# Attention values with the probabilities stationary, the row of maxima by DMA, the attention output token-major

## The reference

```python
s = jnp.einsum('bqkgd,bskd->bkgqs', qblk, k).astype(F32) * scale      # layer 0
p = jax.nn.softmax(s, axis=-1)                                       # layer 1: concatenated with the sink logit
o = jnp.einsum('bkgqs,bskd->bqkgd', p.astype(v.dtype), v)
y_a = o_a.reshape(B, T, A_W) * jax.nn.silu(a_g)
out = jnp.concatenate([y_a, y_b], axis=-1) @ w_out
```

## Time and profile before

| | |
|---|---|
| median of 3 runs | 2318.3 us |
| the profiled execution | 2322.14 us |
| its span, first to last instruction | 2320.3 us |
| mean granted TensorE clock | 0.926 |
| PE / PEld / DVE / ACT / POOL busy | 86 / 57 / 41 / 34 / 7 % |
| attention of layer 0, first scores to the gate's first load | 200.3 to 466 us |
| attention of layer 1, the same | 1192.6 to 1365.9 us |

### The profile page before, as it was taken

How to read it: one execution, slowest core, us unless ns; L and a number is a source line. 1 busy time by engine, 2 the same in 40 slices (tenths; PEclk the granted TensorE clock), 3 DMA queues, 4 the chain that set the end, 5 groups by cost and what they waited for, 6 DMA issues and landing times.

```text
span 2320.3 us, 30145 instructions
## 1 busy us (share of the span) xinstructions
PE 1995.8 (86%) x12212; PEld 1317.6 (57%) x12212; DVE 944.7 (41%) x1899; ACT 784.4 (34%) x1663; POOL 162.1 (7%) x235
## 2 busy tenths in 40 slices
PE   2988999997999988888979998968858868868998
PEld 1654555543555544765657754457457467467476
DVE  1665444212223465234634311562462461552442
ACT  2452444411222224214435531323423423423431
POOL 0000000000000000000000000014014023023000
PEclk8997999998999999998979999969979979979999
DMA  7110000031000242531010021100100100101222
GB/s 284 37 62 14 0 1 1 1 112 55 0 1 1 75 162 83 182 111 66 8 66 1 1 93 60 49 2 9 45 2 17 46 2 18 45 2 49 83 95 100
DMA packets 61292, 118.38 MB, mean 51 GB/s; under 512 B 5048, under 2 KB 27724, under 8 KB 61025
## 3 DMA queue, kind: packets, MB, share of 16 engines
q1 hardware_dynamic: 40033, 57.53, 7.4%
q0 software_dynamic: 8640, 33.75, 4.1%
q10 hardware_dynamic: 12480, 25.17, 3.0%
HBM read 96.47 MB, written 19.96 MB: 50 GB/s over the span
## 4 chain that ended last, share of the span: by engine, by line
PE 75%; DVE 10%; ACT 5%; DMA 3%; POOL 3%; DVEq 2%; issue 1%; ACTq 1%; SPq 0%; PEldq 0%; PEld 0%; POOLq 0%
PE ps L1757 8%; PE ps L535 8%; PE ps L833 8%; PE ps L1001 5%; PE ps L944 5%; PE ps L1328 3%; PE ps L1168 3%; PE ps L1353 3%; PE ps L1169 3%; PE ps L1170 3%; PE ps L788 2%; PE ps L1945 2%; PE ps L815 2%; PE ps L814 2%; PE ps L802 2%; DVE work L2045 2%
## 5 line engine op out<-in xcount | busy, mean ns | idle before, releaser
L833 PE MATMUL ps<-work 128*128 128x512 f32 (+3 forms) x512 | 232.5, 537 | 0.0
L857 DVE TENSOR_REDUCE work<-ps 128x1 f32<-128x512 f32 (+2 forms) x272 | 145.4, 561 | 201.5 <-PE ps L788 200.8
L907 ACT ACTIVATE work<-ps 128x512 f32<-128x512 f32 (+3 forms) x256 | 132.1, 517 | 195.7 <-PE ps L815 141.9
L1757 PE MATMUL ps<-hT,wring 128*128 128x512 f32 (+1 forms) x576 | 191.0, 494 | 8.0 <-SPq L2110 5.6
L535 PE MATMUL ps<-wring,hT 128*128 128x512 f32 (+2 forms) x576 | 193.0, 493 | 0.0
L814 PE MATMUL ps<-qA,kA 128*128 128x512 f32 (+3 forms) x256 | 172.3, 673 | 2.2 <-ACT work L898 1.8
L1757 PEld LDWEIGHTS ps<-hT,wring 128*128 128x128 f32 x576 | 96.2, 193 | 104.3 <-issue 100.2
L535 PEld LDWEIGHTS ps<-wring,hT 128*128 128x128 f32 x576 | 109.1, 192 | 78.5 <-issue 70.3
L1001 PE MATMUL ps<-wring,hT 128*128 128x512 f32 x288 | 127.5, 605 | 5.3 <-SPq L1547 3.4
L944 PE MATMUL ps<-hT,wring 128*128 128x512 f32 (+1 forms) x384 | 126.9, 492 | 4.0 <-DVEq L184 4.0
L788 PE MATMUL ps<-kA,qA 128*128 128x128 f32 (+3 forms) x336 | 101.6, 353 | 27.1 <-DVE work L857 14.8
(11 more groups left out here) (291 smaller groups left out, 3497.1 us busy)
## 6 DMA issues: line engine op xcount, KB each, us to landing
work<-in_w_mod ACTq DMA_DIRECT2D x10, 2048.0 KB, 13.4
work<-in_x_sample SPq DMA_DIRECT2D x16, 512.0 KB, 7.7
wring<-in_w_in_even POOLq DMA_DIRECT2D x4, 2048.0 KB, 8.9
out_y_sample<-work SPq DMA_DIRECT2D x16, 512.0 KB, 3.0
work<-out_y_sample SPq DMA_DIRECT2D x16, 512.0 KB, 4.8
wring<-in_w_in_odd POOLq DMA_DIRECT2D x3, 2048.0 KB, 8.8
wring<-in_w_in_odd POOLq DMA_DIRECT2D x12, 512.0 KB, 6.5
yA_gated<-work SPq DMA_DIRECT2D x8, 576.0 KB, 3.3
```

Source lines behind the costliest of these rows:

```text
L833: pe.matmul(ps[:, 5 + c_, (qa - q0) * P:(qb - q0) * P], vaug[:, h // 4, kt, :], pT[i % 3][:, 0:(qb - qa) * P], start=(first and l == 0), s ...
L857: v.tensor_reduce(dst, src, AX.X, ALU.max).then_inc(sm("mx_used"), 1)
L907: act.activation(pT[i % 3][:, 0:n], ps[:, ST_BANKS[i % len(ST_BANKS)], 0:n], ACT.Exp, scale=0.125).then_inc(sm("p_done"), 1)
L1757: mm = pe.matmul(ps[:, PROJ_BANK[n], 0:m], w[:, k, b * P:(b + 1) * P], hT[:, k, o:o + m], start=(k == 0), stop=(k == KD - 1))
```

## The change

The groups of query tiles become 3, 3 and 3. In "values" the operands change places: each 128 by 128 block of probabilities is stationary and the 64 values with one column of ones move, so that a product of n query tiles becomes n matmuls of 65 columns, and the output is token-major with the sum in column 64. DVE takes the reciprocal and multiplies; ACT's Ln and Exp go. In layer 1 the sink's exponential is computed by ACT from `a_nm` (128 by 9) and added by DVE, and the matmul L831 goes. The nine matmuls of "row" become one transpose of `a_nm`, one copy by ACT to `a_nmT` (9 partitions by 128), and a DMA on SP's queue that writes the nine rows one behind the other into row 64 of `qB`. The row step stands later in a head's list. `yA`, its gate (9 token tiles, 512 columns of weights moving), its DRAM copy and f_ya are token-major; fin transposes 8 blocks of 128 instead of 4 for each tile and has two pairs of banks for the result instead of three.

```diff
-        CHUNKS = [(0, 4), (4, 8), (8, 9)]
+        CHUNKS = [(0, 3), (3, 6), (6, 9)]
...
-            spread = per - (4, 6)[l]
+            spread = per - (6, 7)[l]
             for m in range(MU[l]):
                 yield "max", 0, m
-            for r in range(3):
+            for r in range(1 + l):
                 yield "row", 0, r
...
-                        elif spread < p <= spread + 3:
+                        elif spread < p <= spread + 1 + l:
                             yield "row", h + 1, p - spread - 1
...
+        def att_sp(sp, l):
+            base = l * len(PRODUCTS[0])
+            for h in range(8):
+                sp.wait_ge(sm("row_out"), 8 * l + h + 1)
+                if h >= 2:
+
+                    sp.wait_ge(sm("s_ps"), base + last_product(l, h - 2) + 1)
+                sp.dma_start(qB[h % 2][HD:HD + 1, :].bitcast(F32), a_nmT[h % 2][0:NT, :].bitcast(F32)).then_inc(sm("rows_in"), 16)
...
-                    pe.wait_ge(sm("nm_done"), 8 * l + h + 1)
-                    if r == 2:
-                        pe.wait_ge(sm("row_out"), 3 * (8 * l + h) + 1)
-                    for t in range(*ROW_TILES[r]):
-                        mm = pe.matmul(ps[HD:HD + 1, (MU[l] + r) % 2, (t - ROW_TILES[r][0]) * P:(t - ROW_TILES[r][0] + 1) * P],
-                                       a_nm[h % 2][:, t:t + 1], ident, start=True, stop=True)
-                    mm.then_inc(sm("row_ps"), 1)
+                    if r == 0:
+                        pe.wait_ge(sm("nm_done"), 8 * l + h + 1)
+                        pe.transpose(ps[0:NT, ROW_BANK, 0:P], a_nm[h % 2].bitcast(F32), ident).then_inc(sm("row_ps"), 1)
...
                     if first and c_ == 0:
-                        pe.wait_ge(sm("row_out"), 3 * (8 * l + h) + 3)
+                        pe.wait_ge(sm("rows_in"), 16 * (8 * l + h + 1))
...
                     pe.wait_ge(sm("p_done"), base + i + 1)
-                    if first and l == 1:
-
-                        pe.matmul(ps[:, 5 + c_, 0:(q1 - q0) * P], sumrow[ES, :], qB_plain[h % 2][ES, q0 * P:q1 * P],
-                                  start=True, stop=False, skip_group_check=True)
-                    pe.matmul(ps[:, 5 + c_, (qa - q0) * P:(qb - q0) * P], vaug[:, h // 4, kt, :],
-                              pT[i % 3][:, 0:(qb - qa) * P], start=(first and l == 0), stop=last,
-                              skip_group_check=True).then_inc(sm("pv_ps"), 1)
+                    for j in range(qa, qb):
+                        mm = pe.matmul(out_tile(c_, j - q0), pT[i % 3][:, (j - qa) * P:(j - qa + 1) * P], vaug[:, h // 4, kt, 0:OW],
+                                       start=(first and j == qa), stop=last, skip_group_check=True)
+                    mm.then_inc(sm("pv_ps"), 1)
...
-                    v.wait_ge(sm("ri_done"), 3 * (8 * l + h) + c_ + 1)
-                    v.tensor_tensor(yA[HD * (h % 2):HD * (h % 2) + HD, h // 2, q0 * P:q1 * P], ps[0:HD, 5 + c_, 0:(q1 - q0) * P],
-                                    a_ri[(3 * h + c_) % 2][0:HD, 0:(q1 - q0) * P], ALU.mult).then_inc(sm("y_done"), 1)
+                    nt = q1 - q0
+                    rc = a_rc[c_][:, 0:nt]
+                    v.wait_ge(sm("pv_ps"), base + last_product(l, h, c_) + 1)
+                    o = ps[:, 5 + c_, 0:nt * OW].rearrange("p (j n) -> p j n", n=OW)
+                    den = o[:, :, HD]
+                    if l == 1:
+
+                        v.wait_ge(sm("es_done"), h + 1)
+                        v.tensor_tensor(rc, den, a_es[h % 2][:, q0:q1], ALU.add)
+                        v.drain()
+                        den = rc
+                    v.reciprocal(rc, den)
+                    v.drain()
+                    v.tensor_tensor(yA[:, q0:q1, HD * h:HD * h + HD], o[:, :, 0:HD], rc.unsqueeze(2).to_broadcast([P, nt, HD]),
+                                    ALU.mult).then_inc(sm("y_done"), 1)
...
-                for k in range(KD):
-                    mm = pe.matmul(ps[:, n % 2, 0:m], w[:, k, b * P:(b + 1) * P], hT[:, k, o:o + m], start=(k == 0), stop=(k == KD - 1))
+                for k in range(KD):
+                    mm = pe.matmul(ps[:, t % 2, :], hT[:, k, t * P:(t + 1) * P], w[:, k, :], start=(k == 0), stop=(k == KD - 1))
...
-            sp.dma_start(f_yT[t % NF][:, 0:QW].rearrange("p (b n) -> p b n", b=4),
-                         yA_dram[:, :, t * P:(t + 1) * P].rearrange("b p n -> p b n")).then_inc(d, 16)
+            sp.dma_start(f_ya[t % NF], yA_dram[t * P:(t + 1) * P, :]).then_inc(d, 16)
...
-                for k in range(4):
-                    mm = pe.transpose(ps[:, t % 2, k * P:(k + 1) * P], f_y[t % NF][:, k * P:(k + 1) * P], ident)
+                for b, rows in enumerate((f_ya, f_y)):
+                    for k in range(4):
+                        mm = pe.transpose(ps[:, 2 * (t % 2) + b, k * P:(k + 1) * P], rows[t % NF][:, k * P:(k + 1) * P], ident)
...
-                    act.activation(f_yh[t % 2][:, 0:QW], f_yT[t % NF], ACT.Copy)
-                    act.wait_ge(sm("yT_ps"), NT * l + t + 1)
-                    act.activation(f_yh[t % 2][:, QW:D], ps[:, t % 2, :], ACT.Copy).then_inc(sm("yT_high"), 1)
+                    act.wait_ge(sm("yT_ps"), NT * l + t + 1)
+                    act.activation(f_yh[t % 2].rearrange("p (a n) -> p a n", a=2), ps[:, 2 * (t % 2):2 * (t % 2) + 2, :], ACT.Copy).then_inc(sm("yT_high"), 1)
```

More of the change, by code:

```diff
@@ L450, in backbone @@
         vaug = qr.take(2 * 10 * P).rearrange("p (g t n) -> p g t n", g=2, n=P)
-        yA = qr.take(4 * T).rearrange("p (b t) -> p b t", b=4)
+        yA = qr.take(NT * QW).rearrange("p (t n) -> p t n", n=QW)
         at_qkv = qr.at
@@ L472, in backbone @@
         qB = [take_rounded(ar2, f"qB{i}", T) for i in range(2)]
-        qB_plain = [Region(qB_at + i * T).take(T) for i in range(2)]
-        ES = slice(96, 97)
-        pT = [ar2.take(512) for _ in range(3)]
+        pT = [ar2.take(3 * P) for _ in range(3)]
         a_part = ar2.take(3 * NS)
         a_mx = ar2.take(NT)
-        a_nm = [ar2.take(NT) for _ in range(2)]
-        a_ri = [ar2.take(512) for _ in range(2)]
+        a_nm = [take_rounded(ar2, f"a_nm{i}", 16)[:, 0:NT] for i in range(2)]
+        a_nmT = [take_rounded(ar2, f"a_nmT{i}", P) for i in range(2)]
+        a_es = [ar2.take(NT) for _ in range(2)]
+        a_rc = [ar2.take(4) for _ in range(3)]
         ident_r = take_rounded(ar2, "ident_r", P)
         window_r = take_rounded(ar2, "window_r", 3 * P)
-        k_out = ar2.take(P)
-        assert ar2.at - P >= qr.at
-        sumrow = ar2.take(P)
+        ar2.at = max(ar2.at, qr.at + P)
+        k_out = work[:, ar2.at - P:ar2.at]
         def heads(ap, g=2):
@@ L708, in products @@
                 for c_, (qa, qb) in enumerate(CHUNKS):
[L709 to L712, removed]
-                    else:
-                        of = [(CTX, qa, qb)] + [(k, max(k - 1, qa), min(k + 2, qb)) for k in range(max(qa - 1, 0), min(qb + 1, NS))]
+                    qs = min(qb, NS)
+                    if l == 0:
+                        of = [(k, qa, qs) for k in range(NS + 1)]
+                    else:
+                        of = [(CTX, qa, qs)] + [(k, max(k - 1, qa), min(k + 2, qs)) for k in range(max(qa - 1, 0), min(qs + 1, NS))]
+                    if qb > NS:
+                        of.append((PROMPT_KEYS, NS, NT))
                     out += [(h, k, a, b, c_, i == 0, i == len(of) - 1) for i, (k, a, b) in enumerate(of)]
@@ L764, in masked, with out_tile @@
             return l == 1 and kt not in (CTX, PROMPT_KEYS)
-        ROW_TILES = [(0, 4), (4, 8), (8, 9)]
+        ROW_BANK = 1
+        assert all(m % 2 == 1 for m in MU)
+        OW = HD + 1
+        def out_tile(c_, j):
+            return ps[:, 5 + c_, j * OW:(j + 1) * OW]
+        def att_sp(sp, l):
[5 more added lines that the diff above has]
+                sp.dma_start(qB[h % 2][HD:HD + 1, :].bitcast(F32), a_nmT[h % 2][0:NT, :].bitcast(F32)).then_inc(sm("rows_in"), 16)
         def att_pe(pe, l):
@@ L886, in att_act @@
                     if r == 0:
-                        if h >= 2:
[L889 to L899, removed]
+                        act.wait_ge(sm("row_ps"), 8 * l + h + 1)
+                        if 8 * l + h >= 2:
+                            act.wait_ge(sm("rows_in"), 16 * (8 * l + h - 1))
+                        act.activation(a_nmT[h % 2][0:NT, :], ps[0:NT, ROW_BANK, 0:P], ACT.Copy).then_inc(sm("row_out"), 1)
+                    else:
+                        if h >= 2:
+                            act.wait_ge(sm("y_done"), 3 * (8 * l + h - 1))
+                        act.activation(a_es[h % 2], a_nm[h % 2].bitcast(F32), ACT.Exp, scale=0.125,
+                                       bias=sinks[:, h:h + 1]).then_inc(sm("es_done"), 1)
                 elif what == "scores":
@@ L956, in gateA_act @@
             mod_load(act, f"gateA{l}")
[L957 to L962, removed]
+            for t in range(NT):
+                act.wait_ge(sm("gA_mm"), NT * l + t + 1)
+                if t >= 2:
```

(5 more changed lines are left out.)

72 lines of the change are left out of this document (27 added, 45 removed).

## The result

The changed kernel takes 2449.7 us (median of 4, 2446.7 to 2457.8) against 2318.2: a ratio of 1.0575, 95% interval 1.0549 to 1.0601. It is slower by 131 us, where 59 us faster was forecast. Where further down one kernel has executions at widely different times, the slow ones also have a lower mean granted clock, and the ratios leave them out.

A forecast was written before the change was run, and what follows sets the result against it. PE was taken as the bound, holding 75% of the chain of waits. Layer 0 -28, layer 1 -39 and fin +8 gave -59 us, from the profiled 2322.1 to 2263, median 2259; range 2238 to 2292.

The forecast's parts named there:

- the clock falls in the attention: Rival, chance 0.05: in half of a head PE streams 65 columns in the time of 128, so the clock might drop.
- My two arguments against the rival: Attention: PE stays without gaps, and layer 1's many small passes run at 0.97 clock.
- The sign I had named: Attention: forecast wrong if the clock falls below 0.9, value loads stand over 0.14 apart, or PE waits over 1 us for the row.
- The rival's price: Half clock: about 11.5 us a layer 0 head, 9 in layer 1, 160 in all; a loss from 37% of the attention.
- The further gain: Chance 0.05: value passes at half clock in each first head cost no more, so the kernel gains further.
- Value passes at full clock: Attention values: 0.111 us per 65-column pass, set by the load; 0.107 to 0.166; +0.5 us a head in layer 0, +0.2 in layer 1.
- Heads: Attention: about 30.5 us a head in layer 0 and 16.9 in layer 1; in sum -28 and -39 us.
- The transpose's wait: Row step: PE's transpose waits for DVE's `nm_done`, 0.85 us a head in layer 0, 0.6 in layer 1; ends 0 and 1.5.
- Waits for DVE before the max units: Layer 0: PE's 18.1 us behind ACT's reciprocal, 2.5 us a head, all taken as gone; at worst 1 stays.
- The row DMA: After the transpose: 2.65 us, hidden behind 3.2 us of PE work in layer 0, 3.9 in layer 1; slow-DMA rival 0.01.
- Fin: Four more transposes a tile, 0.43 us each tile, 18 tiles: +7.9 us; tiles of 12.0 us.
- Theory A: Experiments' theory: layer 0 never leaves its low entry clock, since value passes stream 65 columns in a 128-column load's time.

The follow-up runs named there:

- the second experiment: Changed kernel with 128 moving value columns in head 0 of layer 0 only, 65 in all other heads: 2251.6 us, 0.9720 of before.
- 128-column kernel: Changed kernel with value matmuls moving 128 columns (64 values, 64 ones) instead of 65 in all heads: 2252.3 us, 0.9728 of before.
- The row part: Kernel before plus only the transpose, ACT copy and row DMA (second DMA for layer 1's sink row), values with 512 columns: 2281.2 us, 0.9857.
- the extra matmuls in the opening: Changed kernel plus one unused 512-column matmul after each of 25 max units in layer 0's opening: 2250.7 us in one execution, 2449.7 in the other.
- the swap alone: Changed kernel with the nine row matmuls and ACT copies of before, no row DMA: 2286.5 us, 0.9874; one execution took 2357.9.
- a standstill of 13.6 us: Twelve small DMAs before head 3's row DMA in layer 0: 2389.2 us with 128 columns in head 0 only, 2266.8 with 128 in all heads.

## Why the prediction was wrong, step by step

- **The step that failed is the clock.** The sum took every pass at its full-clock price, and the rival "the clock falls in the attention" got 0.05. I had asked whether 65 columns would make a full clock fall; they don't (layer 1, and the seven later heads of layer 0 in the second experiment). But layer 0 enters at half clock, which the earlier trace rows showed for the opening, and the question was whether the new mix would bring it up. In the changed kernel's four executions it did not. My two arguments against the rival were true and beside the point: PE stayed without gaps (busy 438.45 of 439.20 us) at half clock, and layer 1's high clock said nothing of layer 0. The sign I had named, a clock below 0.9 in the attention, is what came.
- **The rival's price was wrong too.** I wrote that at half clock the scores and max units double and "the values stay", since I took the load's 0.11 us for independent of the clock. It is 0.21 at half clock. A head takes 55.9 us, not the 42 of that rival; eight heads lose 8 x 25.4 = 203 us, so that layer 0 alone turns the forecast gain of 59 into a loss once 29% of it (59/203) runs at half clock. The further gain that I gave 0.05, value passes that cost no more at half clock, falls with it.
- **Value passes at full clock: right.** 0.111 was taken, 0.11 measured (0.67 us for six). The load sets the pace, and load and stream overlap. The Trainium skill, "TensorE: Matmul & The Clock Gate", in the part on packing small matmuls, lets a load overlap only where row groups differ; these 65-column passes disagree with it as the 128-column ones did: one after the other they would take 0.166 by the prediction's estimate. A few lines earlier the same part of the Trainium skill names the background weight buffer as a second case in which a load is pulled ahead, and that would fit these passes.
- **Heads: right where the clock is up.** 30.5 us in layer 0 with 128 columns (30.5 forecast), 16.5 in layer 1 (16.9). By stage the 128-column kernel's attention of layer 0 takes 264.5 us, 25 less than before (28 forecast); layer 1's, in the changed kernel, 45 less (39).
- **The transpose's wait** was taken too long, 0.85 and 0.6 us; in the 128-column kernel's layer 0 PE waited 2.3 us in seven heads, 0.33 each, and in the changed kernel's layer 1 0.2. Waits for DVE before the max units went from 18.1 us to 1.6, as forecast. Both rows from the 128-column kernel, layer 0:

```profile
PEld ps L815 <- DVE a_nm L878: 2.3, 7, 0.3
PEld ps L803 <- DVE work L863: 1.6, 7, 0.2
```

- **The row DMA: right.** In the changed kernel's opening it is bare: transpose at 194.36, ACT at 194.84, issue at 195.13, scores at 197.22, 2.86 us for 2.65 forecast; later heads don't wait for it. The pause mattered, but not through its length.

```profile
194.36 0.09 PEld L815 LDWEIGHTS ps<-con,a_nm 128*9 128x9 f32 x1 [1.85 <-DVE a_nm L878]
194.84 0.27 ACT L910 ACTIVATE a_nmT<-ps 9x128 fp32r<-9x128 f32 x1 [22.13 <-PE ps L815]
195.13 0.90 SPq L781 DMA_DIRECT2D qB<-a_nmT  x1
197.22 0.29 PEld L825 LDWEIGHTS ps<-qA,kA 128*128 128x128 f32 x1 [2.76 <-DMA qB<-a_nmT]
```

- **Fin: half right.** In layer 1 the eight transposes hold the tile's first matmul back 1.00 us, where four took 0.55; tiles start 12.0 us apart, 12.0 forecast, +3.6 for the stage. In layer 0 the stage became 2.6 us shorter instead of 4 longer; that the loads of 2 KB rows shorten its waits fits, but no run isolates it. The changed kernel, PEld timeline:

```profile
2369.03 1.03 PEld L1152 LDWEIGHTS ps<-con,work 128*128 128x128 f32 x8
2370.03 0.19 PEld L1169 LDWEIGHTS ps<-hT_r,f_yh 128*128 128x128 f32 x1
```

- **The row part** alone brought 33 us for 44. By stage in its trace, layer 0's attention became 18.5 us shorter (19.8 expected, a head 31.57 us instead of 34.25) and layer 1's 18.9 (24.5), so the term that was too large is layer 1's. There this kernel has a second row DMA, and PE waits 3.7 us for it in the opening.

**When the clock rose.** Layer 1's first products also run at 0.50, and it has 65 columns, yet it comes up. The traces show why this is no counterexample. The changed kernel, the first products of layer 0, then those of layer 1 to the first value pass, and what follows:

```profile
197.20:200.20 3.00, 2.98 (x9) 2.79 (x10) 1.14 (x2) 0.98 (x2) 0.00 (x0) 0.50 0.02 5
1358.80:1363.40 4.60, 4.60 (x17) 4.60 (x18) 1.25 (x2) 1.34 (x3) 0.00 (x0) 0.51 0.00 0
1363.40:1365.00 1.60, 1.60 (x15) 1.60 (x14) 0.69 (x1) 0.34 (x2) 0.00 (x0) 1.00 0.00 0
```

In layer 1 PE runs scores, mask and max matmuls for 4.60 us before the first value pass, at 1363.40, and the clock rises just before that. In layer 0, which has no mask, the value passes begin after 2.9 us, at 200.16, with the clock still at 0.50, and there it stays. With six wide matmuls in the pause the clock also rose before a value pass, and with the old row matmuls during the first scores behind them, at 199.8. The one trace in which it rose among 65-column passes is that of the extra matmuls in the opening: during the first six, behind 3.0 us of scores and max matmuls, and this is the kernel whose other execution stayed down. All this is read from one trace each; no run takes the mask matmuls out of layer 1 or makes layer 0's first products longer.

Open: why one execution of a program takes one way and another the other (the opening with extra matmuls, the swap alone). Theory A is shown as far as this: with 65 columns throughout and no wide matmuls added ahead of the first products, eight of eight executions stayed down (the changed kernel and the one with six 65-column matmuls in the pause), and with three wide ones four of four; with 96 or 128 columns in the first group or more, or six wide matmuls in the pause, none of 21 did.

## What to carry to other kernels

When an edit narrows the moving operand of most matmuls, look first at the granted clock with which the stage is entered, and ask whether the new work can raise it, not only whether it would let it fall; a busy PE is no answer. Where the load of weights sets the pace, useless columns up to the width of the load were free here (30.50 us a head with 65 and with 128) and can be worth far more than the work they add. A few wide matmuls in a wait that is there anyway are a cheap guard; check it over several executions, since one program here went both ways, and one run proves nothing.

## What the runs showed of the hardware

- The granted clock stayed at 1.2 GHz for 439 us while PE was busy for 438.45 of them, and in gate A, with 512 columns moving, it was up from some 640 us on.
- Loads of weights follow the clock: 0.11 us for 128 by 128 at 2.4 GHz, 0.21 at 1.2.
- Both levels can last under the same 65-column stream of a head: 30.5 or 55.9 us a head.
- In a standstill of 13.6 us the clock fell from 1.00 to 0.50; it was back at 1.00 within 6 us of the first scores with 128 columns and not in the rest of the attention with 65.
- A DMA of nine pieces of 512 B within SBUF, issued by SP, let PE go on 2.1 us after its issue.
